# Expert queries, scores and choices moved into the expert stage, head by head

## The reference, cut to what matters

```
x = layer_norm(alpha*x + g_a*mix);  h = x*(1+sc_f) + sh_f
for each block of 128 tokens, each of 8 heads:
    q = h @ wq                                  # two halves of 128 per head
    s = q . keys                                # 2 lists of 128 scores per token
    top 16 of each list; 16 x 16 sums; top 16 of these -> 16 experts, softmax g
    act = gelu(h . u_tab[expert])               # 16 rows of table u per token
    y  += (g*act) . v_tab[expert]               # 16 rows of table v per token
```

## Time and profile before

| what | value |
|---|---|
| median of 3 runs | 8248.79 us (8219.63 to 8254.27) |
| the profiled execution | 8244.72 us |
| its span in the trace | 8242.9 us |
| mean granted TensorE clock | 0.845 |
| busy: PE, DVE, POOL, ACT | 71%, 51%, 35%, 23% |
| moved by the indirect DMAs (queue q0) | 1342 MB of 1669 MB |

### The profile page before, as it was taken

How to read it: one execution, slowest core, us unless ns; L and a number is a source line. 1 busy time by engine, 2 the same in 40 slices (tenths; PEclk the granted TensorE clock), 3 DMA queues, 4 the chain that set the end, 5 groups by cost and what they waited for, 6 DMA issues and landing times. The chain is left out here.

```text
span 8242.9 us, 103239 instructions
## 1 busy us (share of the span) xinstructions
PE 5891.0 (71%) x37056; PEld 4219.6 (51%) x37056; DVE 4219.7 (51%) x8975; ACT 1926.3 (23%) x3578; POOL 2855.2 (35%) x2928
## 2 busy tenths in 40 slices
PE   4876889868567766766657769797767576766774
PEld 3765889748543322332256659795667232322331
DVE  2358232362347766666535562325431666667665
ACT  1345111221112222222115431112201122222221
POOL 0110000110037777777601100001000677777774
PEclk7988999879788888888879889897788788888887
DMA  5110112001559999999820102110142899999996
GB/s 194 39 36 25 55 49 93 22 9 63 215 205 410 403 383 388 386 385 390 347 79 33 38 22 82 62 62 11 44 160 89 337 391 389 389 379 389 387 391 266
DMA packets 458076, 1669.03 MB, mean 202 GB/s; under 512 B 48360, under 2 KB 100776, under 8 KB 445612
## 3 DMA queue, kind: packets, MB, share of 16 engines
q0 software_dynamic: 368640, 1342.34, 42.0%
q1 hardware_dynamic: 86222, 311.41, 10.3%
q10 hardware_dynamic: 2880, 10.49, 0.3%
HBM read 1643.95 MB, written 25.35 MB: 203 GB/s over the span
## 5 line engine op out<-in xcount | busy, mean ns | idle before, releaser
L1503 PE MATMUL ex_ps_y<-ex_v,ex_diag 128*128 128x512 f32 x5120 | 2391.6, 631 | 1072.9 <-ACT ex_diag L1483 1072.9
L1503 PEld LDWEIGHTS ex_ps_y<-ex_v,ex_diag 128*128 128x128 f32 x5120 | 1033.1, 204 | 2432.8 <-issue 1292.2
L1461 DVE CUSTOM_DVE_ANT_0 ring<-ring,ex_h 128x1024 f32<-128x1024 f32 x1280 | 1568.0, 1226 | 930.5 <-DMA ring<-in_peer_u,ex_i 894.0
L1397 POOL DMA_INDIRECT ring<-in_peer_u,ex_i x1280 | 1339.4, 1046 | 445.6 <-issue 437.0
L1397 POOL DMA_INDIRECT ex_v<-in_peer_v,ex_i x1280 | 1261.1, 985 | 390.3 <-issue 390.3
L1483 ACT ACTIVATE ex_diag<-ident,ex_w 128x128 f32<-128x128 f32 x1280 | 487.5, 398 | 1472.6 <-PE ex_ps_y L1503 1426.2
L838 POOL TENSOR_TENSOR rec_k<-rec_k,rec_bounds 128x256 f32<-128x256 f32 x80 | 69.7, 872 | 1015.9 <-ACT rec_k L827 1015.8
L466 POOL MEMSET conv_u<- 128x8 f32 x2 | 0.2, 113 | 1081.0 <-POOLq L79 1081.0
L632 POOL TENSOR_TENSOR att_qs<-att_q,ring 128x512 f32<-128x512 f32 x16 | 20.2, 1263 | 955.5 <-DMA att_lam_in<-in_lam 812.4
L1479 ACT ACTIVATE ex_act<-ex_dot 128x16 f32<-128x16 f32 x80 | 17.3, 216 | 1188.6 <-DVE ex_dot L1461 1188.6
L107 DVE TENSOR_TENSOR mg_wl<-ring,mg_wh 128x2048 fp32r<-128x2048 f32 (+1 forms) x54 | 111.0, 2056 | 351.7 <-ACT mg_wh L209 351.6
(11 more groups left out here) (323 smaller groups left out, 13227.0 us busy)
## 6 DMA issues: line engine op xcount, KB each, us to landing
ring<-in_mod_w SPq DMA_DIRECT2D x36, 2048.0 KB, 9.8
ring<-in_w_in SPq DMA_DIRECT2D x36, 2048.0 KB, 12.5
ring<-in_w_branch SPq DMA_DIRECT2D x12, 2048.0 KB, 7.8
ring<-in_w_in SPq DMA_DIRECT2D x40, 512.0 KB, 4.6
ring<-in_w_in SPq DMA_DIRECT2D x20, 1024.0 KB, 9.1
ring<-in_peer_u,ex_i POOLq DMA_INDIRECT x1280, 5.9
ex_v<-in_peer_v,ex_i POOLq DMA_INDIRECT x1280, 6.3
ring<-in_peer_wq SPq DMA_DIRECT2D x6, 2048.0 KB, 7.8
```

What stands on the lines that cost most here:

```text
L1397: nc.gpsimd.indirect_dma_start(rows[slot], None, table, bass.IndirectOffsetOnAxis(ap=idx_now[j][:, s:s + 1], axis=0)).then_inc(arrived[slo ...
L1461: V.tensor_tensor_reduce(out=row, in0=row, in1=h_now[:], scale=1.0, scalar=0.0, op0=ALU.mult, op1=ALU.add, accum_out=dot[j][:, s:s + 1]).t ...
L1503: last = nc.tensor.matmul(ps_y[:, c:c + 512], diag[s % DIAGS][:], v_row[s][:, c:c + 512], start=False, stop=False)
```

## The change

What the new kernel does, part by part:

- `experts` takes over the queries and scores. Units run by head first (unit n is head n // 5, block n % 5). For each head SP loads 1 MB of query weights; ACT and DVE split it (`high`, `low`). PE computes the queries of blocks 0 and 1, then 2 and 3, then 4 of a head in three jobs (`ask`: 48 matmuls of 256 columns, or of 128 for block 4). A job stands in PE's order before row 3 of unit n, for unit n+4. ACT copies the result out (`turn`) after its ninth diagonal of the unit. PE computes the two score lists of unit n+4 before row 12 of unit n (`score`), and `choose` reads them from PSUM.
- The u rows and the v rows have 8 slots each. POOL issues 16 u rows and then 16 v rows for each unit. A pair of v rows s, s+1 waits until all but 8 of the rows before it are used by PE. The index copy on POOL is gone, and there are 8 diagonals. All 40 units are written out, with no hardware loop.
- PE sums one unit in PSUM, with two buffers. DVE adds each unit's sum to y (`gather_sum`).
- h stays in SBUF, so "h_out" and "h_in" are gone, and so are `peer_queries` and `expert_scores`.
- `first_norm` replaces ln1 and "ht": its x, gains, biases and the first two modulation chunks are loaded during `output_projection` (`aside`); it has four weight buffers, and the transposes stand between the chunks. The first modulation of the program uses six buffers. DVE adds the modulation bias once at the end, in three operations.
- In ln2 SP instead of ACT stores x.

The diff, cut to its core:

```diff
+                if aside is not None:
+                    sp.wait_ge(side_in, aside(sp, side_in))
...
+                for i in range(2, MOD_CHUNKS):
+                    if i >= n:
+                        sp.wait_ge(tile_done, i - n + 1)
+                    sp.dma_start(bufs[i % n][:], mod_weights(T, l, i)).then_inc(w_loaded[i % n], 16)
...
+def first_norm(nc, l, T, y_tok, x_tok, gb, early, h_tok, h_split, x_to, ring, ident):
...
+                for i in range(2, MOD_CHUNKS):
+                    if i >= 4:
+                        sp.wait_ge(tile_done, i - 3)
+                    sp.dma_start(bufs[i % 4][:], mod_weights(T, after, i)).then_inc(w_loaded[i % 4], 16)
+                mod.store(sp, T, after, summed, rows_out)
...
+                for i in range(4):
+                    chunk(i)
...
+                    turn(b)
+                    chunk(4 + b)
...
+        U_SLOTS = V_SLOTS = DIAGS = 8
...
+            return n // NB, n % NB
+
+        def query_job(n):
+            h, b = where(n)
+            return 3 * h + b // 2
...
-                with pool.Fori(0, NB * pairs) as i:
-                    for j in range(2):
-                        n = 2 * i + j
-                        pool.wait_ge(routed, n + 1)
-                        nc.gpsimd.tensor_copy(idx_now[j][:], index[:, bass.ds(TOPK * n, TOPK)]).then_inc(idx_ready, 1)
-                        for rows, arrived, used, table, go in ((u_row, u_in, u_used, T["peer_u"], 2), (v_row, v_in, v_used, T["peer_v"], 4)):
-                            for s in range(TOPK):
-                                slot = s % len(rows)
-                                if s % go == 0:
-                                    pool.wait_ge(used, TOPK * n + s + go)
-                                    if s == 0 and rows is u_row:
-                                        pool.wait_ge(idx_ready, n + 1)
-                                    pool.sem_inc(going, 1)
-                                nc.gpsimd.indirect_dma_start(rows[slot], None, table, bass.IndirectOffsetOnAxis(
-                                    ap=idx_now[j][:, s:s + 1], axis=0)).then_inc(arrived[slot], 16)
+                def gather(rows, arrived, table, n, s):
+                    slot = s % len(rows)
+                    nc.gpsimd.indirect_dma_start(rows[slot], None, table, bass.IndirectOffsetOnAxis(
+                        ap=index[n % 4][:, s:s + 1], axis=0)).then_inc(arrived[slot], 16)
+
+                for n in range(units):
+                    pool.wait_ge(routed, n + 1)
+                    for s in range(0, TOPK, 2):
+                        if TOPK * n + s >= U_SLOTS:
+                            pool.wait_ge(u_used, TOPK * n + s + 2 - U_SLOTS)
+                        pool.sem_inc(going, 1)
+                        for j in (s, s + 1):
+                            gather(u_row, u_in, T["peer_u"], n, j)
+                    for s in range(0, TOPK, 2):
+                        if TOPK * n + s >= V_SLOTS:
+                            pool.wait_ge(v_used, TOPK * n + s + 2 - V_SLOTS)
+                        pool.sem_inc(going, 1)
+                        for j in (s, s + 1):
+                            gather(v_row, v_in, T["peer_v"], n, j)
...
+                def gather_sum(n):
+                    h, b = where(n)
+                    dve.wait_ge(v_used, TOPK * (n + 1))
+                    if h == 0:
+                        V.tensor_copy(y_tok[:, b, :], ps_y[n % 2][:]).then_inc(y_out, 1)
+                    else:
+                        V.tensor_tensor(y_tok[:, b, :], y_tok[:, b, :], ps_y[n % 2][:], ALU.add).then_inc(y_out, 1)
...
+                choose(0)
+                low(1)
+                choose(1)
+                for n in range(units):
...
+                    if n + 2 < units:
+                        choose(n + 2)
+                    if n:
+                        gather_sum(n - 1)
+                    if b == NB - 1 and h + 2 < PH:
+                        low(h + 2)
+                gather_sum(units - 1)
...
+                        act.activation(diag[s % DIAGS], ident[:], ACT.Copy, scale=wgt[n % 2][:, s:s + 1]).then_inc(diag_ready, 1)
+                        if s == TOPK // 2:
+                            if n + 4 < units and where(n + 4)[1] % 2 == 0:
+                                turn(n + 4)
+                            if b == 2 and h + 2 < PH:
+                                high(h + 2)
...
+                    for a in range(2):
+                        w_cols, toks = slice(a * P, (a + 1) * P), slice(b * P, b * P + width)
+                        for k in range(KT):
+                            for m, (w, x) in enumerate(((w_high, 0), (w_high, 1), (w_low, 0))):
+                                last = nc.tensor.matmul(ps_q[:, a, 0:width], w[h % 2][:, k, w_cols], h_split[x][:, k, toks],
+                                                        start=k == 0 and m == 0, stop=k == KT - 1 and m == 2)
...
+                    pe.wait_ge(v_in[s % V_SLOTS], (l * units + n) * 32 + 16 * (s // V_SLOTS + 1))
+                    pe.wait_ge(diag_ready, TOPK * n + s + 1)
...
+                ask(0)
+                pe.wait_ge(loaded, 48)
+                score(0)
+                score(1)
+                ask(2)
+                score(2)
+                score(3)
+                for n in range(units):
+                    if n >= 2:
+                        pe.wait_ge(y_out, n - 1)
+                    for s in range(TOPK):
+                        if s == 3 and n + 4 < units and where(n + 4)[1] % 2 == 0:
+                            ask(n + 4)
+                        if s == TOPK - 4 and n + 4 < units:
+                            score(n + 4)
+                        sums(n, s)
...
+                def aside(sp, sem):
+                    for b in range(NB):
+                        sp.dma_start(x_tok[:, b, :], rows(b)).then_inc(sem, 16)
+                    for j, row in enumerate(("ln_g", "ln_b")):
+                        sp.dma_start(gb[:, j, :], T[row][bass.ds(l, 1), 0, :].to_broadcast([P, D])).then_inc(sem, 16)
+                    for i in range(2):
+                        sp.dma_start(early[i][:], mod_weights(T, bass.ds(l + 1, 1), i)).then_inc(sem, 16)
...
-                    q_t = inner.enter_context(nc.sbuf_tensor("peer_q", [P, 2 * PH, TOK], F32))
-                    peer_queries(nc, l, T, h_split, q_t, ring)
-                    expert_scores(nc, l, T, q_t, scores)
-                with ExitStack() as inner:
-                    h_tok = inner.enter_context(nc.sbuf_tensor("h_tok2", [P, NB, D], F32))
-                    copy_rows(nc, "h_in", [(h_tok[:], T["h_rows"].rearrange("(b p) n -> p b n", p=P))])
-                    experts(nc, l, T, h_tok, y_tok, scores, ident, u_in, v_in, ring)
+                    merged_split = split_tensor(inner, "merged")
+                    split_activation(nc, "ms", main, merged_split)
+                    output_projection(nc, l, T, merged_split, y_tok, ring, aside)
+                if stop == "mix": return
+                h_split = split_tensor(peer, "peer_h")
+                h_tok = peer.enter_context(nc.sbuf_tensor("h_tok", [P, NB, D], F32))
+                first_norm(nc, l, T, y_tok, x_tok, gb, early, h_tok, h_split, rows, ring, ident)
+                experts(nc, l, T, h_split, h_tok, y_tok, early, small, ident, u_in, v_in, ring)
...
```

More of the change, by code:

```diff
@@ L267, in silu, with multiply @@
         act.activation(self.csilu[:, :, 0:2], self.cond[:], ACT.Silu).then_inc(silu_done, 1)
[L269 to L279, removed]
+    def multiply(self, i, weights):
+        for k in range(KT):
+            for g in range(MOD_GROUPS):
+                last = self.nc.tensor.matmul(self.psum[32 * g:32 * (g + 1), i * P:(i + 1) * P], self.csilu[:, k, :],
+                                             weights[:, k, g * P:(g + 1) * P], start=k == 0, stop=k == KT - 1)
+        return last
     def clear(self, pool, zeroed):
@@ L283, in clear, with add_bias, store @@
         self.nc.gpsimd.memset(self.csilu[:], 0.0).then_inc(zeroed, 1)
[L285 to L290, removed]
+    def add_bias(self, summed):
+        for j in range(3):
+            bank = self.rows[:, 4 * j:4 * j + 4, :].rearrange("p a n -> p (a n)")
+            self.nc.vector.tensor_tensor(bank, self.psum[:, 512 * j:512 * (j + 1)], bank, ALU.add).then_inc(summed, 1)
+    def store(self, sp, T, l, summed, rows_out):
+        sp.wait_ge(summed, 3)
         for mine, row in self.strips(lambda c: T["mod_rows"][l, c]):
@@ L1219, in residual_norm @@
         stats, mv, root, nbias = sb("stats", [P, NB, 12]), sb("mv", [P, NB, 2]), sb("root", [P, NB]), sb("nb", [P, NB])
[L1220 to L1224, removed]
+        with stage(nc, f"{name}_in", f"{name}_dve", f"{name}_var", f"{name}_root", f"{name}_xd", f"{name}_out") as (
+                block, (loaded, dve_steps, var_done, root_done, x_done, stored)):
```

(23 more changed lines are left out.)

345 lines of the change are left out of this document (191 added, 154 removed).

## The result

The changed kernel takes 8552.7 us (median of 4 runs, 8543.1 to 8557.0), the kernel before 8251.5 (4 runs, 8219.6 to 8257.0). The ratio is 1.037, with a 95% interval from 1.034 to 1.040: slower by 301 us. The forecast was 8416, with 8200 to 8620 for 8 times in 10. All comparisons use fast runs; one run of the kernel before, beside the first four experiments, took 15070 us and is left out as slow.

What follows compares the result with a forecast made beforehand. No engine bounded the whole program; in the expert stage DMA was always busy and POOL at its limit. Forecast: 2 x (-191 + 160 + 128) - 23 = +171, 8416 us, with 8200 to 8620 for 8 in 10.

Steps and rivals of the forecast that it cites:

- The stages: Before each layer's first expert fetch: 113.7 us instead of 306.3; with small later terms, 191 us less per layer.
- The first modulation: Once, at the program's first modulation: six buffers and earlier first chunks save 23 us (12 to 25).
- The mechanism of the cycle: From T, a unit's last dot's start: POOL's v14 waits for PE's eighth used row, delaying the next u rows queued behind.
- The size of the plain cycle: Expert unit without query job: 47.1 us instead of 43.0, 39 times, +160 us per layer (+80 to +265).
- The 15 rows: In a unit's cycle, the last u row follows the first 15 rows later, taking 19.4 us.
- With less competition: Assumption for u rows in the expert cycle: POOL issues them at the v rows' pace, 1.29 us each.
- u0's issue: POOL issues the next unit's first u row at T + 21.6, after v14 at 19.0 and two rows of 1.29.
- The query jobs: 22 jobs per layer before row 3 each shift v14 and the next T by 5.8 us: +128 us (105 to 177).
- The drained queue: Rival for expert fetches: POOL's waits idle the DMA engines, rows land in 4.4 us, cycle 45.1, 8256 us; chance 0.22.
- Interference: Rival: POOL and DVE hinder each other, 1.99 us per row issue, landings reach 7.3, cycle 49.8, 8626 us; chance 0.20.
- The hidden queries: Rival: query jobs fit PE's idle 13 us per unit, removing 256 us: 8160 us; chance 0.08.

Runs made afterwards that it cites:

- the first four experiments: In the study's order: eight v slots alone; query job later; POOL's queues in halves; the last two edits together: ratios 1.070, 1.008, 0.965, 0.969.
- before_8: The kernel before with only its v rows changed, to 8 slots asked for in pairs: 8814.6 us, ratio 1.070.
- halves: Changed kernel, POOL taking v rows 0-7, next unit's u rows 0-7, v rows 8-15, next u rows 8-15, still 8 slots each: 7948.7 us, ratio 0.965.
- after_psum: Changed kernel with the unit's h copied by ACT to PSUM for the dots, scores in one bank three units ahead: 8505.9 us, ratio 1.033.
- late_ask: Changed kernel with the query job before row 9 instead of row 3: 8302.8 us, ratio 1.008.
- halves_psum: The kernel of halves with the edit of after_psum, h of the unit in PSUM: 7829.4 us, ratio 0.951.
- psum_late: halves_psum with the job before row 9 and ACT's copy and weight part behind the last diagonal: 8201.5 us, ratio 0.956; repeated: 7831.0, 0.951.

## Why the prediction was right, and where its size was off

The measured time lies in the range, in its upper part, and the slowdown is 301 us where 171 were forecast.

**The stages: right.** 116.5 us from the start instead of 306.3 to the first fetch, where 113.7 was worked out; with the 1.4 us that come behind it -188.4 per layer (forecast -191). The first modulation gave -21.0 (forecast -23).

**The mechanism of the cycle: right.** PE starts at T + 2.5, and POOL's waits end on PE's row sums. v14 at 19.6 (19.0 predicted), u0 at 22.1 (21.6). before_8 shows that the slots do it without any other part of the change. halves shows the reverse: the same slots with another order in the queue lose nearly all of the cost.

**The size of the plain cycle: the term that was mis-sized.** A unit without job and load takes 48.8 us instead of 47.1, and the same 1.7 us is in every cycle: 1.7 x 78 = 133 us. The ten units with a load take 2.1 us more, about 20 us in all, and the jobs cost 5 less than forecast. That is +148 us; with 7 from the stages and the modulation, and the 27 us elsewhere against it, it comes to 128, where the difference is 127 us between the profiled +298 and the forecast's +171. The terms are:
- The 15 rows, + 1.4 (20.8 for 19.4), the term that failed most. "With less competition" was an assumption: units of the kernel before need 20.6 us from first to last dot, and the changed kernel the same. The prediction's own rows said so (3028.86 - 3008.21 = 20.65 us in the earlier trace rows). With that number in place of 19.4 the same sum gives about 8510 us. The rows of single units lie between 19.0 and 23.0. after_psum puts 0.7 of the 1.7 us on DVE holding POOL, by the same units without job and load (48.8 against 48.1 us); what makes the rest isn't settled.
- u0's issue, + 0.4 (22.0 for 21.6), nearly all from v14. Its landing without a load is 6.1 us, as assumed (6.2).
- The loads. A step was missing: the weights of the heads, 1 MB each, which the changed kernel loads inside the stage, and which the prediction counted nowhere. u0's landing is 8.9 us in the mean of the 10 units with such a load in front of it and 6.1 in the others (5.8 before, and 9.1 against 6.0 in late_ask). Part of it is caught up by later rows, so that the cycle grows by 2.1. No run moved these loads, so this cause is argued. The longest landings are 7.3 in the kernel before and 7.9 in before_8, which have no such loads, and 10.2 and 9.9 in the changed kernel and in late_ask; but halves has the loads and stays at 8.9.

**The query jobs: right.** The right neighbour is a unit without a load: 54.5 - 48.8 = 5.7 us a job (forecast 5.8), 22 of them 125 us (forecast 128). The 48 matmuls of 128 columns take 5.6 us from first to last start, and those of 256 columns 5.7 to 6.0: the middle of the bounds 2.9 to 11.9 held. late_ask shows that place, not work, is the price.

**The rivals.** The drained queue is false: the share fell to 0.87 as expected, and yet the median landing is 6.3, not 4.4. For a DMA from GpSimd the Trainium skill (page "DMA: Bandwidth & Descriptors", section "Anatomy of one DMA") states a fixed 2.0 us and the bytes at 436 GB/s. Worked out from that as an estimate, 512 KB take 3.2 us, or 4.1 with the 0.93 us of the issue; the shortest landing in the trace, 4.1, agrees, and the gaps in the queue didn't bring the others there. Interference was given as a cycle of 49.8, and the cycle is 49.4, or 48.8 without a load. So that rival's number (8626) is nearer to the result than the forecast's, by cycle and by median. Its pace of the rows, 1.39 us, is what came (20.8 / 15), but its landing of 7.3 did not, and DVE holding POOL makes only 0.7 of the 1.7 us; that the total comes near is in part luck. The Trainium skill (page "SBUF — State Buffer", section "Who interferes with whom") says that a DVE instruction with two SBUF inputs contends with a GpSimd instruction that reads SBUF. The runs agree, a fetch taking its indices from SBUF: with one input in PSUM the u rows' issue goes from 1036 to 937 ns, and in the halves it is worth 144 us. The hidden queries are false where the job stands, and true in late_ask and in the halves.

The prediction named what stands behind v14 on POOL as the reason for the loss. It did not draw the conclusion that the order in the queue, and not the eight slots, is what costs: in the order of halves the same change is a gain of 3.5%, and with one input of the dots in PSUM of 4.9%.

## What to carry to other kernels

Here fewer buffers cost almost nothing by themselves: with eight v slots in halves the v rows wait 38 us for PE in the whole run, and the rest of that cycle is POOL's own issue. What costs is which instructions stand in the same in-order queue behind the wait for a free one. Find the release that comes last, list what is queued behind it, and put first what the next unit needs first. Work on an engine that is idle a quarter of the time isn't free if it stands ahead of the instruction that releases somebody's buffer; six rows later it was. Take a term from the rows of the same instruction where there are any, not from its neighbour: the u rows' own pace was in the trace. Count every load that a change puts beside a stage of fetches: fetches behind a load of 1 MB landed 3 us later.

## What the hardware showed unexpectedly

- A fetch issued by POOL takes 0.93 to 0.94 us when DVE leaves it alone. Beside a dot with two SBUF inputs most still take about 0.95, but some are held, up to 1.99 us (23% over 1.1 us in the changed kernel, 33% in halves); beside the subtraction of `low` they take up to 3.0. A dot with one input in PSUM doesn't hold it: 0.95 us at most in 1193 cases.
- 48 fp32r matmuls take nearly as long with 128 columns (5.6 us) as with 256 (5.7 to 6.0).
- A fetch's median landing did not fall when the DMA engines had gaps: 6.3 us at a share of 0.87, 6.1 at 1.01. At the same share of 1.01 it was 7.4 in halves_psum, where POOL issues faster. So the share alone doesn't tell the landing.
- Beside psum_late the kernel before took 8587 us, and 8231 to 8252 beside all others. The ratio of the improved kernel differed too, by 0.005. The record gives the same chip number for it as for halves_psum, where it took 8231, so that neither the chip nor its state then is shown as the cause.
